# Four edits to a one-core inference step: order in two attention heads, a merged 448-column projection, and own keys placed behind the cached ones with values used in fp32

## The chip, the cores and the metric

The kernel runs on one core of a Trainium2 chip. The metric is the device time of one execution in microseconds (us). The engines are named as in the profile: PE is TensorE (PEld its weight loads), DVE is VectorE, ACT is ScalarE, POOL is GpSimd, SP is SyncE, which issues nearly all DMAs.

## The reference

One step of a two-layer streaming encoder over 512 prompt tokens and 8 running streams of 16 new tokens each (640 tokens together), width 1024, all in fp32. What matters here:

```python
# layer A, gated linear attention, 4 heads: q, k of 128, v and gate of 256 columns
q, k, v, gate, glr = split(rmsnorm(x, norm_pre) @ w_in)
g = log_sigmoid(glr @ w_gate2 + b_gate) / 16
S, o = gla_core(q * DK**-0.5, k, v, g, S0)   # chunks of 64: b = cumsum(g); (q e^b)(k e^-b)^T, causal, @ v; plus q e^b @ S
x = x + rmsnorm((rmsnorm(o, head_norm) * silu(gate)) @ w_out, norm_post)
# shared latent of layer B
lat = rmsnorm(x, kv_norm) @ kv_w_down             # 1024 x 320
ckv, krope = rmsnorm(lat[:256]), rope(lat[256:])  # keys: 512 cached + 16 own per stream
# layer B, latent attention, 8 heads
q_lat, gate = split(rmsnorm(x, norm_pre) @ w_in)  # 384 and 1024 columns
q = rmsnorm(q_lat, q_norm) @ w_uq                 # 128 + 64 rotary per head
x = x + rmsnorm((softmax(q k^T * scale + mask) v * silu(gate)) @ w_out, norm_post)
```

Outputs are the two results, the recurrent states, and the latent and rotary rows.

## The kernel before

Everything is fp32-accurate by splitting: a value x is kept as a pair, hi (x rounded to fp32r) and lo (x - hi), and a product is three matmuls, hi·hi + lo·hi + hi·lo. The helper `mm3` issues them (lines 1563 to 1565). ACT usually makes the hi half with a copy (helper `copy`, line 991) and DVE the lo half with a subtraction (helper `low`, line 1260); POOL makes some lo halves and scales weights by their norm gains.

The program is one hand-ordered list of steps, written by `steps()`, `project_out`, `latent_layer` and `samples`. `PARTS` says which engines have a part in a step, and every engine runs its parts in the order of the list, one behind the other; nothing overtakes. A wait, `after(engine, other, step)`, stands in front of a part. PE's results go to eight PSUM banks in rotation, and a step waits until the reader of the bank's last contents is done. Weights and cached rows come by SP's DMAs through a ring of stages of 1024 columns (4, and 6 in the samples; `share_stages`), in the order of `STAGED`; SP waits in order until a stage's last reader is done. A `piece` is one such load with its hi and lo copies.

Steps that the change and the prediction touch:

- Layer A, head h: `c` cumulative gates (PE), `q`, `k` projections, `kT` transposes of k (PE; its other parts write kn), `sc` scores, `U` state products of the prompt, `o` and `os` outputs of prompt and streams (os has 16 small products with the stream states), `Us` state products of the streams with a DVE add into `st_s` and ACT scalings of it, `gl(t)` output gates of the last head, `oT(t)` transposes of the gated rows. In head 0 the step `lgh(u)` makes the pair of the log gates `lg`.
- Layer B: `lc` latents (320 columns), slab `ql0` with steps `qa`, `qas` (256 columns of q_lat), slab `kq` with steps `kq`, `kqs` (64 rotary key columns and the other 128 of q_lat), `gb` gates, `cT` latent transposes.
- Samples, stream b: `ct`, `cr`, `cs` bring the cached latents transposed, the cached rotary keys and the cached latents by rows. `ss(b)` is the scores, the reduction for the maximum (DVE) and the exponentials (ACT); own keys of all streams are one block of 128 columns, where a 0 / minus-large mask product leaves only the stream's 16. `st(b)` transposes the probabilities, `sv(b)` multiplies them with the latent rows (256 columns, 5 blocks of 128 keys), `cx(b)` transposes the result. In the list, loop b holds st(b), the loads of b+3, ss(b+2), cx(b-1), sv(b).

Of the kernel before, what the change touches and what calls it, by code (L numbers as in the profile page):

```python
# [93 lines left out]
SLAB_AT["v0g"] = 3  # L94
PITCH = {name: 2 * VG if name == "v0g" else PIECE for name in SLABS}
# [22 lines left out]
def steps():  # L118
# [49 lines left out]
def project_out(out, load, ph):  # L168
# [18 lines left out]
    for t in range(NT + 4):  # L187
# [10 lines left out]
        if t == NT + 1:  # L198
            load("ql0")
# [31 lines left out]
def prompt_heads(out, load):  # L231

    for h in range(-1, HB):
        if h >= 0:
# [15 lines left out]
        if 0 <= h < 4:  # L250
            load(("hd", h + 4))
        elif h == 4:
            out += [("ct", 0), ("cr", 0)]
        elif h == 5:
            out += [("ct", 1), ("cr", 1)]


def samples(out, load):

    for b in range(SB):  # L260
        out += [("st", b)]
# [16 lines left out]
        out += [("sv", b)]  # L278
# [199 lines left out]
def program(nc, dram, outs):  # L478
# [14 lines left out]
    with ctx:  # L493
# [101 lines left out]
        cn_s = pair("cn_s", [P, KL])  # L595
# [15 lines left out]
        for i in range(NSTAGE, NWIDE):
            place[0] = qlT_at + 4 * D * (i - NSTAGE + 2)
            stage.append(sb(f"stage{i}", [P, PIECE]))
# [17 lines left out]
        spT = pair("spT", [P, TOK])  # L631
# [17 lines left out]
        sk_at = block_at[6], block_at[1]  # L649
        skS = [put(sk_at[i], f"skS{i}", [P, PAST], fp32r) for i in range(2)]  # L650
        skL = [put(sk_at[i] + 4 * PAST, f"skL{i}", [P, PAST], fp32r) for i in range(2)]
        sT_hi = [put(block_at[(5, 7)[i]], f"sT_hi{i}", [P, KC, PAST], fp32r) for i in range(2)]
        sT_lo = [put(block_at[(4, 0)[i]], f"sT_lo{i}", [P, KC, PAST], fp32r) for i in range(2)]
        cn_hi = [put(block_at[2 + i], f"cn_hi{i}", [P, PAST // P, KL], fp32r) for i in range(2)]
        cn_lo = [put((qN_at, kN_at)[i], f"cn_lo{i}", [P, PAST // P, KL], fp32r) for i in range(2)]
# [1262 lines left out]
```

How the kernel before makes its waits and increments, by code:

```python
        def after(eng, who, *step):  # L727
            eng.wait_ge(done[who], AT[who][step])
# [43 lines left out]
        @block.sync  # L773
# [58 lines left out]
                        load_stage(n)  # L832
                elif kind == "const":
                    sp.dma_start(const_raw[:, :], dram["const_r"]).then_inc(const_r_in, 16)
                elif kind == "lds":
                    h = step[1]
                    if h == 0:
                        sp.dma_start(post[:, :], dram["a_norm_post"].to_broadcast([P, D])).then_inc(post_in, 16)
                        sp.dma_start(lat_gain[:, :], dram["kv_latent_norm"].unsqueeze(0).to_broadcast([P, KL])).then_inc(post_in, 16)
                    if h:
                        sp.wait_ge(state_out, 16 * h)
                    else:
                        after(sp, "pe", "c", HA - 1)
# [18 lines left out]
                    after(sp, "dve", "r", "A", t)  # L864
                    sp.dma_start(kept[:, t, :], x1[:, t, :]).then_inc(kept_out, 16)
                elif kind == "ldk":
                    after(sp, "pe", "sv", SB - 1)
                    sp.wait_ge(kept_out, 16 * NT)
                    sp.dma_start(xB[:, :, :], kept).then_inc(rest_in, 16)
                elif kind == "och":
# [11 lines left out]
                    sp.dma_start(y_prompt[0, t * P:(t + 1) * P, :] if t < NP else y_sample.rearrange("b l d -> (b l) d"),  # L883
                                 xB[:, t, :]).then_inc(y_out, 16)
            sp.wait_ge(y_out, 16 * NT)
            sp.wait_ge(latent_out, 16 * 4)
```

## Time and profile before

| | |
|---|---|
| runs, us | 646.52, 646.67, 646.95 (median 646.67) |
| the profiled execution, us | 644.79 |
| its span, us | 643.0 |
| mean granted PE clock | 0.994 |
| PE busy, us | 617.9 (96% of the span) |
| DVE, ACT, POOL busy, us | 383.2, 315.8, 125.3 |
| DMA packets' share of 16 engines | 35.8% |

The span is the time between the first and the last instruction that the profiler saw; the execution's own time is 1.8 us longer. Busy shares are means over stages that have different limits, so each stage is looked at by itself. Matmuls overlap in the records: the time that one takes of PE is the distance from start to start, not its own length.

### The profile page before, as it was taken

The numbers are of one execution on the slowest core, as the hardware profiler recorded it, in microseconds if no ns is written. First come the engines' busy times: TensorE is split into PE (matmuls) and PEld (weight loads), VectorE is DVE, ScalarE is ACT, GpSimd is POOL, SyncE is SP. The second block draws the span as 40 slices with busy tenths as digits, with TensorE's granted clock in tenths as the row PEclk, the third lists the DMA queues.
The fourth block names the chain that finished last, engine by engine and source line by source line (L and its number), as shares of the span: only waits on it lengthen the run. The fifth ranks groups of instructions, "written<-read, shape, count | busy, mean of one in ns | idle before, by whom it ended". The sixth has DMA issues, their size and how long they took to land.

```text
span 643.0 us, 12101 instructions
## 1 busy us (share of the span) xinstructions
PE 617.9 (96%) x4714; PEld 596.3 (93%) x4714; DVE 383.2 (60%) x574; ACT 315.8 (49%) x618; POOL 125.3 (19%) x140
## 2 busy tenths in 40 slices
PE   8998999999999879999999999999999999999996
PEld 7998999999999779999999999989999888899996
DVE  5475667355454674238664567557778877773415
ACT  6786464442462553236435433355555668872311
POOL 0110010010030152216425410211000118650001
PEclk9999999999999989999999999999999999999998
DMA  8923262270262262234234420321001046766004
GB/s 301 345 82 92 90 199 73 87 215 28 74 197 67 74 229 66 86 87 173 67 93 112 127 66 2 114 70 47 34 18 50 13 151 209 252 196 229 2 1 165
DMA packets 66281, 73.69 MB, mean 115 GB/s; under 512 B 8112, under 2 KB 58544, under 8 KB 66096
## 3 DMA queue, kind: packets, MB, share of 16 engines
q1 hardware_dynamic: 66224, 72.91, 35.8%
q8 instruction: 38, 0.62, 0.4%
q14 instruction: 19, 0.16, 0.1%
HBM read 62.12 MB, written 10.78 MB: 113 GB/s over the span
## 4 chain that ended last, share of the span: by engine, by line
PE 65%; DVE 15%; ACT 10%; issue 4%; DMA 3%; POOL 2%; SPq 1%; DVEq 0%; ACTq 0%; POOLq 0%
PE bank L1563 21%; PE bank L1564 20%; PE bank L1565 20%; DVE slab_lo L1260 2%; DMA x_nat<-in_x_sample_dram 2%; ACT prob L1194 2%; DVE pT_lo L1260 2%; ACT slab_hi L991 1%; PE bank L1610 1%; DVE sT_lo L1260 1%; ACT sT_hi L991 1%; ACT qS L991 1%; DVE stat L1540 1%; DMA x_raw<-in_xT_dram 1%; DVE rows L1256 1%
## 5 line engine op out<-in xcount | busy, mean ns | idle before, releaser
L1563 PE MATMUL bank<-slab_hi,hat_hi 128*128 128x256 f32 (+2 forms) x600 | 171.0, 285 | 3.8 <-DVE rows L1423 1.8
L1564 PE MATMUL bank<-slab_lo,hat_hi 128*128 128x256 f32 (+2 forms) x600 | 169.8, 283 | 0.0
L1565 PE MATMUL bank<-slab_hi,hat_lo 128*128 128x256 f32 (+2 forms) x600 | 169.8, 283 | 0.0
L1563 PEld LDWEIGHTS bank<-slab_hi,hat_hi 128*128 128x128 f32 x600 | 115.2, 192 | 5.0 <-DVE rows L1423 2.0
L1564 PEld LDWEIGHTS bank<-slab_lo,hat_hi 128*128 128x128 f32 x600 | 115.2, 192 | 0.0
L1565 PEld LDWEIGHTS bank<-slab_hi,hat_lo 128*128 128x128 f32 x600 | 115.2, 192 | 0.0
L1260 DVE TENSOR_TENSOR slab_lo<-stage,slab_hi 128x1024 fp32r<-128x1024 f32 (+3 forms) x70 | 84.8, 1212 | 24.9 <-ACT slab_hi L991 23.4
L1563 PE MATMUL bank<-hat_hi,slab_hi 128*128 128x320 f32 x256 | 79.8, 312 | 0.9 <-DVE rows L1487 0.8
L1565 PE MATMUL bank<-hat_hi,slab_lo 128*128 128x320 f32 x256 | 79.1, 309 | 0.0
L1564 PE MATMUL bank<-hat_lo,slab_hi 128*128 128x320 f32 x256 | 79.1, 309 | 0.0
L991 ACT ACTIVATE slab_hi<-stage 128x1024 fp32r<-128x1024 f32 (+3 forms) x70 | 71.0, 1014 | 10.2 <-issue 3.6
L1563 PEld LDWEIGHTS bank<-hat_hi,slab_hi 128*128 128x128 f32 x256 | 48.1, 188 | 1.4 <-DVE rows L1487 1.4
L1564 PEld LDWEIGHTS bank<-hat_lo,slab_hi 128*128 128x128 f32 x256 | 48.1, 188 | 0.0
L1565 PEld LDWEIGHTS bank<-hat_hi,slab_lo 128*128 128x128 f32 x256 | 48.1, 188 | 0.0
L1565 PE MATMUL bank<-slab_hi,oT_lo 128*128 128x256 f32 x160 | 45.3, 283 | 0.0
L1563 PE MATMUL bank<-slab_hi,qS 128*128 128x256 f32 x128 | 36.5, 285 | 0.0
L1564 PE MATMUL bank<-slab_lo,qS 128*128 128x256 f32 x128 | 36.2, 283 | 0.0
L945 POOL TENSOR_TENSOR stat<-stat,stat 128x1 f32<-128x1 f32 (+1 forms) x8 | 2.3, 287 | 171.4 <-ACT junk L1123 136.3
L1138 ACT ACTIVATE junk<-bank 128x256 bf16<-128x256 f32 x26 | 9.7, 383 | 50.4 <-PE bank L1565 50.4
L971 POOL TENSOR_TENSOR skL<-stage,skS 128x512 fp32r<-128x512 f32 x8 | 14.6, 1827 | 92.2 <-ACT skS L991 92.2
L1565 PEld LDWEIGHTS bank<-slab_hi,oT_lo 128*128 128x128 f32 x160 | 30.7, 192 | 0.0
L1194 ACT ACTIVATE prob<-bank,stat 128x512 f32<-128x512 f32 (+3 forms) x32 | 16.6, 523 | 19.4 <-DVE stat L1521 19.1
(340 smaller groups left out, 1434.2 us busy)
## 6 DMA issues: line engine op xcount, KB each, us to landing
stage<-in_a_w_in_dram SPq DMA_DIRECT2D x22, 512.0 KB, 5.2
stage<-in_b_w_in_dram SPq DMA_DIRECT2D x10, 512.0 KB, 3.8
st_s<-in_state_gla_dram SPq DMA_DIRECT2D x4, 1024.0 KB, 6.7
out_dram<-st_s SPq DMA_DIRECT2D x4, 1024.0 KB, 4.9
stage<-in_a_w_out_dram SPq DMA_DIRECT2D x8, 512.0 KB, 4.3
stage<-in_ckvT_dram SPq DMA_DIRECT2D x8, 512.0 KB, 4.1
stage<-in_cache_ckv_dram SPq DMA_DIRECT2D x8, 512.0 KB, 4.0
stage<-in_b_w_out_dram SPq DMA_DIRECT2D x8, 512.0 KB, 3.5
```

What stands on the lines that cost most here:

```text
L945: link(pool.tensor_tensor(r, s, S1(("rrm",), stat2)[:, t:t + m], MUL))
L971: last = pool.tensor_tensor(skL[b][:, :], staged_as(kind, step), raw(skS[b][:, :]), SUB)
L991: return act.activation(out, in_, ACT.Copy)
L1138: last = act.activation(junk[:, i * 256:(i + 1) * 256], row[:, i * 256:(i + 1) * 256], ACT.Square, accum_out=S1(("y", ph, t), t=s))
L1194: last = act.activation(prob[u][:, c0:c0 + i + 1, :], bank[:, j, 0:(i + 1) * P].rearrange("p (s n) -> p s n", n=P), ACT.Exp, bias=S1(("S", ...
L1256: return dve.tensor_tensor(out, a, b, op)
L1260: return dve.tensor_tensor(lo, full, raw(hi), SUB)
L1540: last = dve.reduce_max(S1(("ss", b), stat2), row[:, 0:TOK], AX.X, negate=True)
L1563: pe.matmul(out, a[0], b[0], start=first, stop=False)
L1564: pe.matmul(out, a[0], b[1], start=False, stop=False)
L1565: return pe.matmul(out, a[1], b[0], start=False, stop=last)
L1610: last = pe.transpose(row[:, k * P:(k + 1) * P], rows[:, t, k * P:(k + 1) * P], ident)
```

## The change

1. Head 0: the log gates' pairs are made ahead of q and k; the qk(1) piece moves behind q; `kT` moves ahead of `c(2)`.
2. Last head: `Us` keeps the PE products and the DVE add, and the ACT scalings become a step `Ux`. The order becomes Us, o, os, gl(2), Ux, gl(3), oT(0), gl(4). The POOL scaling of piece wo A 1 waits for gl(3)'s DVE part.
3. Slabs `ql0` and `kq` and their steps become one slab `krq` of 448 columns, with pieces of two row blocks each in a slab of its own (`slab[4]`), and one step per token tile. k is rotated once for all tiles by a DVE step `kr`.
4. Samples: the stream's own 16 keys are copied behind the 512 cached ones (POOL step `ot`), so the scores are two halves of 264 columns without a mask product. A POOL step `zr` zeroes the last probability block. The exponentials are two ACT instructions. `sv` takes fp32 probabilities and the cached latents in fp32 straight from their stage: one fp32 matmul per block instead of three, and no pairs of them. The ring has 8 stages, and `cs` no longer has an ACT or POOL part.

```diff
 # steps(), head 0
-    ... ("lgh", HA), ("ln", 3), ("lg", 3), ("ln", 1), ("lg", 1)]
-    out += [("g0", 3), ("g0", 4), ("c", 0), ("em",), ("e", 0), ("lgh", 1), ("piece", ("qk", 1), 0), ("q", 0), ("lgh", 2), ("lgh", 3), ("qlo", 0), ("k", 0), ("klo", 0)]
-    out += [("c", 1), ("c", 2), ("kT", 0), ("c", 3)]
+    ... ("lgh", HA), ("ln", 3), ("lg", 3), ("ln", 1), ("lgh", 2), ("lg", 1), ("lgh", 3)]
+    out += [("g0", 3), ("lgh", 1), ("g0", 4), ("c", 0), ("em",), ("e", 0), ("q", 0), ("qlo", 0), ("piece", ("qk", 1), 0), ("k", 0), ("klo", 0)]
+    out += [("c", 1), ("kT", 0), ("c", 2), ("c", 3)]
 # steps(), every head; last = last head
-        out += [("os", h), ("Us", h, 0), ("Us", h, 1), ("sts", h)]
         if last:
-            out += [("o", h), ("ldr",)]
-            out += [("gl", t) for t in range(EARLY_GATE, NT - 1)] + [("oT", 0), ("gl", NT - 1)]
+            out += [("Us", h, 0), ("Us", h, 1), ("o", h), ("os", h), ("gl", EARLY_GATE), ("Ux", h, 0), ("Ux", h, 1), ("sts", h), ("ldr",)]
+            out += [("gl", t) for t in range(EARLY_GATE + 1, NT - 1)] + [("oT", 0), ("gl", NT - 1)]
 # slabs(), latent_layer()
-    out["ql0"] = halves("b_w_in", 0, "b_norm_pre")
-    out["kq"] = [[("kv_w_down", k, k + 4, KL, ROPE, "kv_norm"), ("b_w_in", k, k + 4, 256, QL - 256, "b_norm_pre")] for k in (0, 4)]
+    out["krq"] = [[("kv_w_down", k, k + 2, KL, ROPE, "kv_norm"), ("b_w_in", k, k + 2, 0, QL, "b_norm_pre")] for k in range(0, KD, 2)]
-    out += [("lcn",)]
-    load("kq")
-    out += [("qa",), ("qas",)]
+    out += [("piece", "krq", 3), ("lcn",)]
+    out += [("krq", t) for t in range(2)]
     load(("gb", 3))
-    out += [("kq",), ("kqs",), ("cn",), ("och",), ("qs",)]
+    out += [("krq", t) for t in range(2, NT)] + [("kr",), ("cn",), ("och",), ("qs",)]
 # samples()
-        out += [("st", b)]
+        out += [("st", b)] + [("zr", b + 2)] * (b + 2 < SB)
         if b + 3 < SB:
-            out += [("ct", b + 3), ("cr", b + 3)]
-        if b + 1 < SB:
-            out += [("cs", b + 1)]
+            out += [("ct", b + 3), ("cr", b + 3), ("ot", b + 3)]
@@
-        out += [("sv", b)]
+        out += [("sv", b), ("cs", b)]
 # PE, scores and values of a stream
-                    for o, keys, kr, kl in ((bank[:, 0, :], sT, skS[b % 2][:, :], skL[b % 2][:, :]),
-                                            (bank[:, 1, 0:P], cT_s, krS[:, SEQ:TOK], krL[:, SEQ:TOK])):
+                    for half in range(2):
+                        c0 = half * (KEYS // 2)
                         for c in range(KC):
-                            mm3(o, cut(qab, A_, c, b), cut(keys, A_, c), c == 0, False)
+                            mm3(o, cut(qab, A_, c, b), cut((sT_hi[b % 2], sT_lo[b % 2]), A_, c, keys), c == 0, False)
...
-                        last = mm3(bank[:, 0, 0:KL], cut(spT, A_, slice(s * P, (s + 1) * P)), cut((cn_hi[b % 2], cn_lo[b % 2]), A_, s) if s < NT - 1 else cut(cn_s, A_, A_), s == 0, s == NT - 1)
+                        x = staged_as("cs", ("cs", b))[:, s, :] if s < NT - 1 else cn_s[:, :]
+                        last = pe.matmul(bank[:, 0, 0:KL], spT[:, s * P:(s + 1) * P], x, start=s == 0, stop=s == NT - 1)
 # ACT, exponentials of a stream
-                    last = act.activation(sprob[b % 2][:, :, :], row[:, 0:TOK].rearrange("p (s n) -> p s n", n=P), ACT.Exp,
+                    act.activation(sprob[b % 2][:, 0:NT - 1, :], row[:, FIRST_KEY:FIRST_KEY + PAST].rearrange("p (s n) -> p s n", n=P), ACT.Exp,
...
+                    last = act.activation(sprob[b % 2][:, NT - 1, b * SL:(b + 1) * SL], row[:, FIRST_KEY + PAST:FIRST_KEY + KEYS], ACT.Exp,
 # POOL
+                elif kind == "ot":
...
+                    for to, x in ((sT_hi, cT_s[0]), (sT_lo, cT_s[1])):
+                        pool.tensor_copy(to[b % 2][:, :, PAST:KEYS], x[:, :, mine])
+                    mine = slice(SEQ + b * SL, SEQ + (b + 1) * SL)
+                    pool.tensor_copy(skS[b % 2][:, PAST:KEYS], krS[:, mine])
+                    last = pool.tensor_copy(skL[b % 2][:, PAST:KEYS], krL[:, mine])
```

Where the steps move, the instruction lists show the following. First DVE in head 0, before; `lg_lo` are the log gates' lo halves, `tmp` the scaled q, `slab_lo` the piece, `kt` the scaled k:

```order
L1315 SCALAR_TENSOR_TENSOR rows<-rows,bank 128x256 x2
L1260 TENSOR_TENSOR lg_lo<-z_min,lg_hi 128x512
L1260 TENSOR_TENSOR slab_lo<-stage_49,slab_hi 128x1024
L1342 SCALAR_TENSOR_TENSOR tmp<-bank,Ep 128x640
L1348 COPY q_own<-tmp 128x4x16 x2
L1260 TENSOR_TENSOR lg_lo<-z_min,lg_hi 128x512 x2
L1260 TENSOR_TENSOR qT_lo<-tmp,qT_hi 128x640
L1256 TENSOR_TENSOR kt<-bank,Em 128x640
```

The same place of the changed kernel:

```order
L1284 TENSOR_TENSOR lg_lo<-z_min,lg_hi 128x512
L1339 SCALAR_TENSOR_TENSOR rows<-rows,bank 128x256
L1284 TENSOR_TENSOR lg_lo<-z_min,lg_hi 128x512
L1339 SCALAR_TENSOR_TENSOR rows<-rows,bank 128x256
L1366 SCALAR_TENSOR_TENSOR tmp<-bank,Ep 128x640
L1372 COPY q_own<-tmp 128x4x16 x2
L1284 TENSOR_TENSOR qT_lo<-tmp,qT_hi 128x640
L1284 TENSOR_TENSOR slab_lo<-stage_49,slab_hi 128x1024
L1280 TENSOR_TENSOR kt<-bank,Em 128x640
```

All `lg_lo` now stand ahead of `tmp`, and between `tmp` and `kt` are only the lo halves of q and of the piece. Second, ACT in the last head, before; `st_s` are the stream states, `junk,stat` the squares of os (one) and o (four), `st_in` the gates' tanh:

```order
L1123 ACTIVATE junk,stat<-bank 128x256
L1127 ACTIVATE st_s<-st_s,Ep 128x256 x8
L1121 ACTIVATE junk,stat<-bank 128x256 x4
L1101 ACTIVATE st_in<-bank,stat_68 128x256 x2
L991 ACTIVATE hat_hi<-bank 128x8x128
```

And of the changed kernel:

```order
L1156 ACTIVATE junk,stat<-bank 128x256 x4
L1158 ACTIVATE junk,stat<-bank 128x256
L1136 ACTIVATE st_in<-bank,stat_68 128x256
L1163 ACTIVATE st_s<-st_s,Ep 128x256 x8
L1136 ACTIVATE st_in<-bank,stat_68 128x256
L1020 ACTIVATE hat_hi<-bank 128x8x128
```

The squares stand ahead of the eight scalings, and the tanh of gl(3) behind them. Third, POOL in the samples, before, over three streams; `cn_lo` is the lo half of the cached rows, `skL` that of the cached rotary keys:

```order
L971 TENSOR_TENSOR skL_153<-stage_130,skS_151 128x512
L967 TENSOR_TENSOR cn_lo_161<-stage_49,cn_hi_159 128x1024
L971 TENSOR_TENSOR skL_154<-stage_52,skS_152 128x512
L967 TENSOR_TENSOR cn_lo_162<-stage_129,cn_hi_160 128x1024
L971 TENSOR_TENSOR skL_153<-stage_49,skS_151 128x512
```

And of the changed kernel, over one stream:

```order
L1001 MEMSET sprob_145 128x128
L979 TENSOR_TENSOR skL_157<-stage_131,skS_155 128x512
L989 COPY sT_hi_151<-cT_s_hi 128x2x16
L989 COPY sT_lo_153<-cT_s_lo 128x2x16
L991 COPY skS_155<-krS 128x16
L992 COPY skL_157<-krL 128x16
```

One large instruction of a stream is gone, and a memset and four small copies are added, the copies behind `skL`.

## Rows read from the trace of the kernel before

**Rows 1.** Page, shares of the chain that ended last

```profile
PE 65%; DVE 15%; ACT 10%; issue 4%; DMA 3%; POOL 2%; SPq 1%; DVEq 0%; ACTq 0%; POOLq 0%
```

**Rows 2.** Waits of PE over the span: total, times, longest

```profile
PE bank L1610 <- DVE rows L1423: 4.3, 1, 4.3
PE bank L1563 <- DVE rows L1423: 1.8, 1, 1.8
PE bank L1664 <- DVE kt L1256: 1.2, 1, 1.2
```

**Rows 3.** Table by windows around head 0: window, length, busy (x), clock, DMA

```profile
48.76:55.84 7.08, 7.08 (x50) 7.08 (x50) 3.31 (x6) 4.08 (x9) 0.00 (x0) 1.00 0.10 19
55.84:65.76 9.92, 7.62 (x65) 7.25 (x64) 5.57 (x8) 6.04 (x18) 0.00 (x0) 1.00 0.58 190
```

**Rows 4.** Timeline of DVE in head 0: start, length

```profile
52.61 1.23 DVE L1260 TENSOR_TENSOR slab_lo<-stage,slab_hi 128x1024 fp32r<-128x1024 f32 x1 [0.43 <-ACT slab_hi L991]
...
56.62 1.42 DVE L1260 TENSOR_TENSOR lg_lo<-z_min,lg_hi 128x512 fp32r<-128x512 f32 x2 [1.60 <-ACT lg_hi L991]
58.94 0.82 DVE L1256 TENSOR_TENSOR kt<-bank,Em 128x640 f32<-128x640 f32 x1
```

**Rows 5.** Table by windows in head 3

```profile
212.17:238.60 26.43, 19.94 (x165) 18.30 (x164) 16.64 (x21) 14.12 (x30) 11.27 (x12) 0.94 0.54 185
230.00:232.00 2.00, 2.00 (x10) 2.00 (x11) 1.97 (x2) 0.01 (x1) 1.92 (x2) 0.50 1.01 385
229.96:235.07 5.11, 5.11 (x33) 5.11 (x34) 4.97 (x5) 1.02 (x1) 4.87 (x4) 0.72 1.01 400
235.07:238.60 3.53, 3.53 (x34) 3.41 (x32) 2.71 (x5) 2.81 (x4) 1.11 (x1) 1.00 0.12 48
```

**Rows 6.** Timeline of DVE in head 3

```profile
219.60 2.48 DVE L1256 TENSOR_TENSOR st_s<-bank,st_s 128x1024 f32<-128x1024 f32 x2
...
230.30 2.10 DVE L1256 TENSOR_TENSOR rows<-rows,st_in 128x256 f32<-128x256 f32 x1
```

**Rows 7.** Timeline of ACT in head 3

```profile
220.92 3.45 ACT L1127 ACTIVATE st_s<-st_s,Ep 128x256 f32<-128x256 f32 x8 [4.24 <-DVE st_s L1256]
```

**Rows 8.** Timeline of POOL in head 3

```profile
228.25 7.93 POOL L924 TENSOR_TENSOR stage<-stage,gain_a_head_norm 128x1024 f32<-128x1024 f32 x4 [0.22 <-POOL stat L948]
```

**Rows 9.** Table by windows: products of 256, 192, 320 and 512 columns

```profile
316.00:330.39 14.39, 14.39 (x123) 14.39 (x121) 10.88 (x9) 3.74 (x12) 8.94 (x8) 1.00 0.15 43
330.39:343.77 13.38, 13.38 (x122) 13.38 (x121) 4.26 (x9) 3.74 (x12) 0.00 (x0) 1.00 0.36 93
343.77:350.82 7.05, 7.05 (x50) 7.05 (x49) 3.08 (x12) 4.64 (x10) 5.78 (x7) 1.00 0.47 139
420.83:429.02 8.19, 8.19 (x39) 6.76 (x37) 6.18 (x8) 5.60 (x8) 0.67 (x1) 1.00 0.39 108
```

**Rows 10.** The fp32 products of line 1597: ns min, median, max, first and last start

```profile
L1597 PEld LDWEIGHTS bank<-q_own x4: 190/190/191, 4.2 to 4.8; 128*128 128x128 f32 x4
```

**Rows 11.** Table by windows in the samples

```profile
532.16:579.50 47.34, 44.53 (x327) 41.20 (x326) 35.13 (x50) 38.38 (x57) 29.60 (x14) 1.00 0.73 225
544.54:547.42 2.88, 2.88 (x20) 2.54 (x19) 2.17 (x5) 2.75 (x5) 1.85 (x1) 1.00 0.92 325
```

**Rows 12.** Timeline of ACT in two streams

```profile
551.92 0.71 ACT L991 ACTIVATE spT_hi<-bank 128x640 fp32r<-128x640 f32 x1
...
556.21 0.80 ACT L1229 ACTIVATE sprob<-bank,stat 128x640 f32<-128x640 f32 x1 [0.73 <-DVE stat L1540]
...
557.54 0.71 ACT L991 ACTIVATE spT_hi<-bank 128x640 fp32r<-128x640 f32 x1
```

**Rows 13.** Timeline of DVE in one stream

```profile
554.03 1.23 DVE L1260 TENSOR_TENSOR sT_lo<-stage,sT_hi 128x1024 fp32r<-128x1024 f32 x1
555.29 0.83 DVE L1540 TENSOR_REDUCE stat<-bank 128x1 f32<-128x640 f32 x1
```

**Rows 14.** Timeline of POOL in one stream

```profile
554.52 1.88 POOL L971 TENSOR_TENSOR skL<-stage,skS 128x512 fp32r<-128x512 f32 x1 [1.27 <-ACT skS L991]
```

More of the change, by code:

```diff
@@ L197, in project_out @@
             out += [("rx", t - 1)]
-        if t == NT + 1:
-            load("ql0")
+        if t > NT:
+            out += [("piece", "krq", t - NT - 1)]
         if 0 <= t - 4 < NT:
@@ L608, in program @@
         place[0] = qlT_at
+        slab[4] = pair("slab4", [P, KD * KRQ])
+        assert place[0] <= temp_at
+        kr_raw = thb[:, NT * ROPE:].rearrange("p (t n) -> p t n", n=ROPE)
+        place[0] = qlT_at
         y_rows = sb("y_rows", [P, NT, D])
         sprob = [sb("sprob0", [P, NT, P])]
[L611 to L613 removed]
+        for i in range(2):
+            place[0] = qlT_at + 4 * D * (i + 2)
+            stage.append(sb(f"stage{NSTAGE + i}", [P, PIECE]))
         place[0] = qS_at
@@ L630, in program @@
         place[0] = temp_at
-        spT = pair("spT", [P, TOK])
+        spT = sb("spT", [P, TOK])
         place[0] = prob_at
@@ L647, in put @@
             return sb(name, shape, dt)
[L649 to L655, printed above, removed]
+        wide = 4 * KC * KEYS
+        sT_hi = [put(block_at[(4, 0)[i]], f"sT_hi{i}", [P, KC, KEYS], fp32r) for i in range(2)]
+        sT_lo = [put(block_at[4] + (wide, 3 * wide)[i], f"sT_lo{i}", [P, KC, KEYS], fp32r) for i in range(2)]
+        skS = [put((block_at[4] + 2 * wide, block_at[0] + wide)[i], f"skS{i}", [P, KEYS], fp32r) for i in range(2)]
+        skL = [put((block_at[4] + 2 * wide + wide // 2, qlT_at + 1024)[i], f"skL{i}", [P, KEYS], fp32r) for i in range(2)]
+        assert block_at[4] + 4 * wide <= phase_at and block_at[0] + wide + wide // 2 <= block_at[2] and 1024 + wide // 2 <= 4 * D
+        for i, at in enumerate((qN_at, kN_at)):
+            stage.append(put(at, f"stage{NSTAGE + 2 + i}", [P, PIECE]))
         place[0] = lat_gain_at
@@ L963, in _ @@
                     last = pool.tensor_scalar(r, r, 1.0 / D, EPS, MUL, ADD)
-                elif kind == "cs":
-                    after(pool, "act", *step)
-                    b = step[1] % 2
-                    last = pool.tensor_tensor(cn_lo[b][:, :, :], staged_as(kind, step), raw(cn_hi[b][:, :, :]), SUB)
                 elif kind == "cr":
@@ L1203, in _ @@
                     else:
-                        after(act, "pe", "O", (1, 4)[b])
-                    last = copy(sT_hi[b % 2][:, :, :], staged_as(kind, step))
+                        after(act, "pe", "O", 4 + b)
+                    last = copy(sT_hi[b % 2][:, :, 0:PAST], staged_as(kind, step))
                 elif kind == "cr":
@@ L1516, in _ @@
                     b = step[1]
-                    last = low(sT_lo[b % 2][:, :, :], staged_as("ct", step), sT_hi[b % 2][:, :, :])
+                    last = low(sT_lo[b % 2][:, :, 0:PAST], staged_as("ct", step), sT_hi[b % 2][:, :, 0:PAST])
                 elif kind == "S":
@@ L1725, in _ @@
                     last = pe.transpose(bank[0:ROPE, 1, 0:P], krn[:, t, :], ident)
-                elif kind in ("qa", "qas"):
-                    last = natural(row, "ql0", range(NP) if kind == "qa" else [NP], 256, KD, hat)
-                elif kind in ("kq", "kqs"):
-                    last = natural(row, "kq", [NP] if kind == "kqs" else range(NP), ROPE + QL - 256, KD, hat)
+                elif kind == "krq":
+                    t = step[1]
+                    w = [x[:, 0:KD * KRQ].rearrange("p (k n) -> p k n", n=KRQ) for x in weights("krq")]
+                    for k in range(KD):
+                        if t == 0 and k % 2 == 0:
+                            after(pe, "dve", "piece", "krq", k // 2)
+                        last = mm3(bank[:, 0, 0:KRQ], cut(hat, A_, k, slice(t * P, (t + 1) * P)), cut(w, A_, k), k == 0, k == KD - 1)
                 elif kind == "qT":
```

181 lines of the change are left out of this document (97 added, 84 removed), and 4 rows, old and new, of the table PARTS.

## Prediction

> **What bounds the kernel now.** I read the shares of the chain that ended last first: 65% of it is PE, 15% DVE and 10% ACT [rows 1]. So PE's own work is the bound almost everywhere, and the rest are places where PE waits for a chain through ACT and DVE. The waits of PE say where: 4.3 us and 1.8 us once each for DVE's `rows` in the last head, and 1.2 us for `kt` in head 0 [rows 2]. Then each edited place was read for itself: tables by windows give PE's time of a stretch, timelines of the other engines say what stood in front of the late instruction. Two kinds of gain follow: less PE work (edits 3 and 4) and shorter waits (1 and 2), and I cost them apart.
>
> **Edit 1, head 0.** k's 48 products take 7.08 us, back to back [rows 3]. The next 9.92 us (c(1), c(2), kT, c(3), sc, U) are 9.92 us long for products that, at 0.1 to 0.125 each, are some 7.0 us of work: 30 for c and 5 for kT at about 0.11, 27 for sc and U at 0.12, from the 0.12 of a 256-column product below. So 2.9 us are waits; the row of `kt` is one, 1.2 us. Why `kt` is late is in DVE's timeline: the last product of k is through at 55.84, but DVE first makes two `lg_lo` (1.42 us, from 56.62), then q's lo half, and `kt` starts only at 58.94 [rows 4]. The second wait, ahead of U, comes from ACT: `kn_hi` is queued behind the copies of c(1) and c(2). After the change the `lg_lo` are done ahead of q, where DVE has room, and `kt` can start when k is through, at about 56.15; kT's transposes follow at 57.1, and c(2) and c(3) then lie over the chain kt, kT_hi, kT_lo. The price is that the two `lg_lo` and the earlier q now fall in k0's time, and that the piece's `slab_lo` (1.23 us [rows 4]), which k needs, is behind q. I put 0.1 us of delay to k's start for it. With kT at 57.1, transposes 0.5, c(2) and c(3) 2.3, sc 1.6 and U 1.5, U ends at 63.0 instead of 65.76. Gain 2.8; bounds 1.2 (only the `kt` wait goes) and 2.9 (all waits go).
>
> **Edit 2, last head.** From the first product of os to the first of `y` A are 26.43 us at a mean clock of 0.94 [rows 5]. Off it go the two waits, 4.3 and 1.8, together 6.15. PE's clock is 0.50 (the 1.2 GHz level) at 230 to 232, just after the long wait in which PE did nothing. In the 5.11 us from oT(0) on, 8 transposes and 24 products stand [rows 5]; at 3.53/32 = 0.11 per transpose and 0.12 per product they would be 3.76. So the slow stretch costs 1.35 us, and it goes if the long wait goes. The work left is 26.43 - 6.15 - 1.35 = 18.9.
>
> Why PE waits: ACT makes eight scalings of the stream states (3.45 us from 220.92), and these wait for DVE's adds (2.48 us from 219.60) [rows 6, 7]; only behind them come the four squares of o, POOL's norm chain of 1.9 us and DVE's `rows`, for which oT(0) waits. In the new order the squares come first. Step by step, from 212.17: Us and o take 3.9 us, os 1.6, so squares end near 218.3, POOL's chain near 220.2, DVE's adds also at 220.2 and its five `rows` at 222.4; PE has gl(2) and gl(3), 48 products or 5.8 us, until 223.5, so oT(0) starts without a wait. What is late next is ACT's tanh of gl(3), behind the scalings: gl(2) ends at 220.6, tanh 0.5, scalings 3.45, tanh 0.5, so 225.1, then hat_hi. gl(4) covers PE until 227.2, and the last transposes and the start of `y` may wait some 0.4 to 1.3 us for the hats. So 19.3 to 20.2, a gain of 6.2 to 7.1. I take 6.7. POOL's scaling of the weight piece (7.93 us for four [rows 8]) now starts behind gl(3)'s DVE part. It matters since the add `rows<-rows,st_in` beside it took 2.10 us [rows 6] where the other adds of this size took about 0.43.
>
> **Edit 3, krq.** The 120 products of 256 columns and their neighbours take 14.39 us, 0.120 each; the 120 of 192 columns take 13.38, 0.1115 each [rows 9]. The trace has no product of 448 columns. It has 320 columns (7.05/48 = 0.147) and 512 columns (8.19/36 = 0.2275) [rows 9]. The line between gives 0.147 + 128 x 0.00042 = 0.2006. 120 of those are 24.1, against 27.8: gain 3.7, and I add 0.1 for one change of step less and take 3.8. Bounds: 0.2275 for each (27.3, gain 0.5) would need 448 columns to cost what 512 do, which the step from 256 to 320 columns speaks against; I keep 3.3 to 4.0. The pieces come from the same stages, with ACT and DVE halves of 896 columns; the fourth lands under the first tiles. DVE's work for k moves behind the last tile as one step, and `cT` waits for it; the gb(3) products lie over it, so I cost it at nothing; if the cover were gone it would be about 2 us.
>
> **Edit 4, samples.** Eight loops take 47.34 us, 5.92 each [rows 11]. PE's work in one: scores 2.88 [rows 11], sv 15 x 0.12 = 1.8, st 0.46, cx 0.16, together 5.3. After: scores are 16 products of 264 columns, 0.123 each by the line above, 1.98, so 0.9 less. For sv only the start of the kernel has fp32 products of 256 columns: their loads are at 4.2 to 4.8, 0.20 apart [rows 10], and ten records stand for six products, so two records or about 0.41 to 0.43 per product, five make 2.1: 0.3 more. The work of a loop is then 4.7.
>
> The Trainium skill ("FP8 and Floating Point Precision", TensorE Precision Notes) says that a true fp32 product takes four passes through the array. By that rule a block would cost four times the 0.12 of a fp32r product, 0.48, and sv 2.4; the sum would be 0.3 us longer for each stream that has no cover. The trace's row is lower than that, and it decides.
>
> But PE's work does not set the loop. ACT and DVE do, in their own order: spT_hi (0.71), sT_hi (1.06), then DVE's sT_lo (1.23) and the maximum (0.83), then ACT's exponential (0.80 and a read of 0.2), qab_hi (0.4) and the next spT_hi, 5.62 us later [rows 12, 13]. The change takes 0.12 off the maximum, puts 0.15 on the exponentials (a second ACT instruction with its own read) and lets sT_lo start 0.2 earlier, since spT_lo is gone: about 5.45. cn_hi (1.06) and cn_lo are off this cycle: ACT's cn_hi lay in the time in which ACT waited for the maximum. So a loop gains about 0.2 where the cycle binds, some 0.7 in all; the last two streams have no scores behind them and pay the 0.3 of sv in full, 0.6. I take a gain of 0.1. Bounds: +5.6 (all loops at PE's 4.7 and a little) if the cycle is wrong, and -4, below.
>
> **Sum.** 2.8 + 6.7 + 3.8 + 0.1 = 13.4 off the profiled 644.79 is 631.4. The profiled execution is 1.9 below the median of 646.67, so the median forecast is 633.3.
>
> **Rivals.**
> *B, samples follow PE.* The removal of three pair makings and a DVE instruction frees more than the cycle above says, and most loops fall by 0.4 to 0.5 more, 3 to 4 us: 629.5. For it: all engines have less to do. Against: the four instructions of the cycle all stay.
> *C, own keys come late.* POOL has `skL` of 1.88 us [rows 14] and behind it four copies. The nearest POOL rows of small size are 0.2 to 0.3 us, so about 1.1 for four; PE's ss(b+2) waits for the last one. I find 0.6 us of slack. If the copies are 0.3 dearer each, each loop loses 0.5: 8 x 0.5 = 4, so 637.3.
> *D, the last head gives part back.* DVE's adds into `st_s` now stand ahead of `rows`, and POOL's scaling, beside gl(4)'s add, doubles its time or worse, as the 2.10 us shows; the hats come 2 us later: 635.5. The Trainium skill ("GPSIMD Engine Reference", Specifications) names this contention, for DVE instructions with two SBUF inputs; the row agrees.
> *E, slower.* SP takes its waits in order. The load of piece wo B 0 now waits for sv(0), and the loads of ct(5), cr(5), cs(2), ct(6) are behind it; with cached rows read by PE straight from their stage, a stage is free only after sv(b). If each loop waits for a load issued that late, PE idles from there. To lose all 13.4 us, six to eight loops must each be 1.7 to 2.3 us late. By my order of issues the nearest load, cs(2), lands 1 us early, so this needs an error of 3 us per loop: 648.
> *F, edit 1 or 3 does nothing:* if in head 0 only the `kt` wait goes, 634.9; that is inside the forecast's range.
>
> **How the numbers follow.** Forecast case 0.52, B 0.15, C 0.16, D with F 0.12, E 0.05. The forecast case alone is 631.5 to 635. The range reaches to B below and to C above: 629.5 to 637.3, leaving out E and the far ends of B and C. A measurement of this kernel can tell about 0.2% (1.3 us) from no change. All cases but E are faster by more than that: 0.94; within, 0.02; slower, 0.04.
>
> **What would show it.** In the profile after: in head 0 `kt` starts about 0.3 us behind k's last product and U ends 2.8 us earlier; in the last head no wait over 1 us at oT(0), and a granted clock of 1.00 there; krq has 120 products 0.20 apart; scores of a stream take 2.0 and sv 2.1 us of PE, and the loop stays near 5.45, with PE waiting for ACT's spT. I am wrong if fp32 products are further apart than 0.48, if 448 columns take the time of 512, if PE waits in the samples for `ot` or for a DMA, or if the clock falls in the last head all the same.

## The result and the profile after

The changed kernel took 623.69 us (median of 5, 623.65 to 624.23), the kernel before 646.52 in the same comparison (645.73 to 646.95): a ratio of 0.9649, 95% interval 0.9636 to 0.9663. That is 22.8 us; I had forecast 13.4 and a range that ended at 629.5. The direction is right, the time is outside the range.

The page of the changed kernel: span, busy times, and the granted clock in 40 slices.

```profile
span 621.9 us, 11803 instructions
...
PE 600.5 (97%) x4546; PEld 577.2 (93%) x4546; DVE 370.1 (60%) x573; ACT 307.9 (50%) x616; POOL 111.1 (18%) x173
...
PEclk9999999999999999999999999999999999999999
```

The span fell by 21.1 us, from 643.0. The two traces were then cut at the same places of PE's program, from the first instruction to the last. The numbers are us between these places; the third and fourth columns belong to experiments below.

```
                                before  changed  before+64 B  changed+64 B
start to the end of U, head 0    65.76    62.77        65.81         62.35
to the first product of y A     172.84   162.85       171.70        166.10
to the last transpose of x       71.14    68.29        68.25         70.60
to gb(3,0) (krq, or ql0 and kq)  34.02    30.93        33.84         30.78
to st(0)                        188.39   188.68       188.64        188.80
to so (the samples)              53.30    52.54        52.98         52.79
to the end                       57.54    55.85        55.82         57.21
span                            643.0    621.9        637.0         628.6
```

Two stretches whose products no edit touches, the output product of layer A (to the last transpose of x) and the end, are 2.85 and 1.7 us shorter. That was in no term of the sum. Where it comes from is seen in a table by windows over 20 us of products of 256 columns, the same code in both (y A); (x) counts instructions. The kernel before:

```profile
250.00:270.00 20.00, 20.00 (x169) 20.00 (x168) 6.29 (x7) 7.92 (x24) 5.17 (x3) 1.00 0.17 53
```

The changed kernel:

```profile
250.00:270.00 20.00, 20.00 (x179) 20.00 (x178) 7.21 (x8) 8.82 (x26) 2.22 (x4) 1.00 0.18 47
```

PE is busy throughout in both, at a clock of 1.00. Yet it starts 179 products instead of 169: by their starts they are 0.1133 us apart in the mean instead of 0.120.

**Head 0.** The windows of k and of what follows to U's end, against [rows 3], and DVE's `kt`, against [rows 4]:

```profile
48.53:55.64 7.11, 7.11 (x49) 7.11 (x49) 4.29 (x7) 3.98 (x10) 0.00 (x0) 1.00 0.01 2
55.64:62.77 7.13, 7.13 (x64) 7.02 (x63) 3.36 (x5) 4.35 (x15) 0.00 (x0) 1.00 0.73 229
```

```profile
55.90 0.82 DVE L1280 TENSOR_TENSOR kt<-bank,Em 128x640 f32<-128x640 f32 x1 [0.56 <-PE bank L1583]
```

k's products take the same, what follows 7.13 instead of 9.92 us. `kt` starts 0.26 us behind k's last product.

**Last head.** Windows over the last head, from its first product (now of Us) to the first of `y` A, against [rows 5]; the scalings and the tanh of gl(3) on ACT, against [rows 7]; the adds and the second adds of gl(3) and gl(4) on DVE, against [rows 6]:

```profile
206.46:225.62 19.16, 17.73 (x165) 16.46 (x165) 14.12 (x22) 14.17 (x30) 6.74 (x11) 1.00 0.46 139
218.00:226.00 8.00, 8.00 (x73) 7.88 (x72) 5.74 (x10) 6.62 (x11) 4.26 (x3) 1.00 0.64 203
```

```profile
216.50 3.45 ACT L1163 ACTIVATE st_s<-st_s,Ep 128x256 f32<-128x256 f32 x8
219.98 0.47 ACT L1136 ACTIVATE st_in<-bank,stat 128x256 f32<-128x256 f32 x1
```

```profile
213.65 2.48 DVE L1280 TENSOR_TENSOR st_s<-bank,st_s 128x1024 f32<-128x1024 f32 x2 [1.27 <-PE bank L1583]
...
221.02 0.43 DVE L1280 TENSOR_TENSOR rows<-rows,st_in 128x256 f32<-128x256 f32 x1
...
223.36 0.42 DVE L1280 TENSOR_TENSOR rows<-rows,st_in 128x256 f32<-128x256 f32 x1
```

The last head takes 19.16 us instead of 26.43. The clock is 1.00; no wait over 1 us is left at oT(0) or behind it (one of 1.4 us for `st_lo` ahead of o is new), and ACT's tanh of gl(3) does come right behind the scalings. The add of gl(3) took 0.43 us, not 2.10: POOL's scaling begins at 221.58, behind it. The add of gl(4) took 0.42: it starts 0.1 us ahead of the end of one of POOL's instructions.

**krq.** 120 products of 448 columns:

```profile
300.05:324.85 24.80, 24.80 (x123) 22.53 (x122) 8.79 (x17) 5.88 (x13) 5.16 (x4) 1.00 0.35 93
```

24.80 / 120 = 0.2067 each.

**Samples.** The eight loops, one stream's scores and one stream's values, against [rows 11]:

```profile
513.52:560.09 46.57, 41.75 (x281) 38.12 (x279) 28.10 (x49) 31.97 (x64) 14.08 (x36) 1.00 0.63 211
525.58:527.61 2.03, 2.03 (x18) 2.03 (x17) 1.23 (x4) 1.96 (x3) 0.21 (x1) 1.00 0.99 367
527.90:530.14 2.24, 2.24 (x12) 1.94 (x12) 2.21 (x2) 1.43 (x2) 0.64 (x1) 1.00 1.09 374
```

Scores take 2.03 us and values 2.16 (the window of values is longer by one wait of 0.08). A loop takes 46.57/8 = 5.82 us in the mean, against 5.92. Then ACT at the same place of three loops and its exponential, against [rows 12], DVE's first instruction behind the maximum, POOL's skL and its last copy, and PE's scores that follow it:

```profile
527.64 1.06 ACT L1020 ACTIVATE sT_hi<-stage 128x1024 fp32r<-128x1024 f32 x1
...
531.05 0.69 ACT L1251 ACTIVATE sprob<-bank,stat 128x512 f32<-128x512 f32 x1 [1.69 <-DVE stat L1559]
...
533.26 1.06 ACT L1020 ACTIVATE sT_hi<-stage 128x1024 fp32r<-128x1024 f32 x1
...
538.70 1.06 ACT L1020 ACTIVATE slab_hi<-stage 128x1024 fp32r<-128x1024 f32 x1
```

```profile
532.60 0.42 DVE L1284 TENSOR_TENSOR qab_lo<-bank,qab_hi 128x256 fp32r<-128x256 f32 x1 [1.63 <-ACT qab_hi L1020]
```

```profile
529.50 1.84 POOL L979 TENSOR_TENSOR skL<-stage,skS 128x512 fp32r<-128x512 f32 x1 [3.48 <-ACT skS L1020]
...
531.85 0.20 POOL L992 CAST skL<-krL 128x16 fp32r<-128x16 f32 x1
```

```profile
532.30 0.36 PE L1581 MATMUL bank<-sT_hi,qab_hi 128*128 128x264 f32 x1 [1.46 <-POOL sprob L1001]
```

From one sT_hi to the next are 5.62 us, and to the instruction at that place in the loop after, a piece's slab_hi, 5.44. ACT waits 1.69 us for DVE's maximum and then DVE 1.63 us for ACT's qab_hi: the two wait for each other. PE waits 1.46 us for the copies. The row names the memset `sprob` that stands behind them, but in the program PE waits for the copies, and it starts 0.25 us behind the last one. The waits of PE in this part of the trace, and who released it by the profile:

```profile
PE bank L1581 <- POOL sprob L1001: 2.9, 3, 1.5
PE bank L1581 <- ACT sprob L1253: 2.4, 3, 1.6
```

Two of the three waits put down to ACT also end 0.25 us behind the last copy (537.73 and 544.44). None of PE's waits here is for a DMA.

### The profile page after: what moved, and what is told of

It reads as the page before. It is cut to its first block and busy times, and to the rows that moved or that the text cites. A ratio compares the mean times of both kernels' runs of the same rounds, so it can differ in the third digit from the quotient of the medians.

```text
span 621.9 us, 11803 instructions
## 1 busy us (share of the span) xinstructions
PE 600.5 (97%) x4546; PEld 577.2 (93%) x4546; DVE 370.1 (60%) x573; ACT 307.9 (50%) x616; POOL 111.1 (18%) x173
## 5 line engine op out<-in xcount | busy, mean ns | idle before, releaser
L1581 PE MATMUL bank<-slab_hi,hat_hi 128*128 128x256 f32 (+2 forms) x560 | 160.6, 287 | 2.0 <-DVE hat_lo L1284 1.0
L1582 PE MATMUL bank<-slab_lo,hat_hi 128*128 128x256 f32 (+2 forms) x560 | 159.6, 285 | 0.0
L1583 PE MATMUL bank<-slab_hi,hat_lo 128*128 128x256 f32 (+2 forms) x560 | 159.6, 285 | 0.0
L1581 PEld LDWEIGHTS bank<-slab_hi,hat_hi 128*128 128x128 f32 x560 | 105.3, 188 | 3.8 <-DVE slab_lo L1284 1.4
L1583 PEld LDWEIGHTS bank<-slab_hi,hat_lo 128*128 128x128 f32 x560 | 105.6, 189 | 0.8
L1582 PEld LDWEIGHTS bank<-slab_lo,hat_hi 128*128 128x128 f32 x560 | 105.2, 188 | 0.7
```

Source lines behind the costliest of these rows:

```text
L1581: pe.matmul(out, a[0], b[0], start=first, stop=False)
L1582: pe.matmul(out, a[0], b[1], start=False, stop=False)
L1583: return pe.matmul(out, a[1], b[0], start=False, stop=last)
```

## The experiments

Three questions were open: what makes unchanged products start closer together; whether each edit is worth its term; and what sets the samples' loops. The kernel before was timed beside each group and took 646.98 (644.61 to 648.82), 648.17 (644.55 to 648.20) and 648.24 (646.05 to 648.79). Its mean clock in these executions goes with its time: 0.994 in those of 644.6 to 645.3, 0.987 to 0.990 in those of 645.9 to 647.9, 0.984 to 0.986 in those above 648. The groups e, f and g ran on three different chips; where runs of two groups are compared, a part of the difference may be the chip's.

**Where tiles lie.** Edit 4 made the constants shorter and two small tables longer, so `hat`, `qS`, `oT_lo` and everything behind `junk` moved by 1472 bytes in SBUF, while the slabs stayed. Worked out from the allocations, `hat` lay 0 modulo 128 bytes from the slabs before, and lies 64 modulo 128 now. In a product of 256 columns `hat` is the stationary side and the slab streams. Four kernels have nothing but unused bytes added:

```diff
+        place[0] += 64          # e1 on the kernel before; e3 on the changed kernel
+        place[0] += 32          # e2 on the kernel before; g4 on the changed kernel
         rows_at = place[0]
-        place = [-(-nc.sbuf_base // 64) * 64]
+        place = [-(-nc.sbuf_base // 64) * 64 + 64]      # e4 on the changed kernel: all tiles
```

**e1**, the kernel before with 64 bytes:

> The kernel before, with 64 unused bytes ahead of `rows`, so that `rows`, `hat` and everything behind lies 64 bytes later in SBUF and the weight slabs do not; nothing else is changed. Theory A (addresses): in the changed kernel the 256-column products run 113 ns apart instead of 120 ns because its constants are smaller and so `hat`, qS and oT_lo lie at another offset to the slabs (64 instead of 0 modulo 128 bytes). Then this kernel gets the 113 ns too, and about 7 to 8 us over some 1150 ns-priced groups of products: 638.5 to 639.5 against 646.5. Theory B (the lower spacing comes from less work on DVE, ACT, POOL or from another chip): 120 ns stay, 646.5 within 1 us.

Measured: 638.97 (638.58 to 641.63), ratio 0.9886 (0.9855 to 0.9917). The same window of its trace:

```profile
250.00:270.00 20.00, 20.00 (x179) 20.00 (x178) 8.20 (x8) 7.12 (x18) 3.89 (x3) 1.00 0.21 61
```

**e2**, 32 bytes in the kernel before:

> The kernel before with 32 unused bytes ahead of `rows`. Theory A does not say which offsets are good. If any offset other than 0 modulo 128 gives 113 ns: 639. If only 64 does: 646.5. If an offset that is no multiple of 64 costs more than either: above 646.5. Theory B: 646.5.

Measured: 644.31 (642.25 to 646.66), ratio 0.9953 (0.9933 to 0.9973), and the products with `hat` are 117 ns apart in the median, but 118.3 in the mean. The kernel before has 119.9 in the mean, e1 115.1. So 32 bytes give about a third of what 64 give.

**e3**, the changed kernel put back to distance 0:

> The changed kernel with 64 unused bytes ahead of `rows`, which puts `hat`, qS and oT_lo back to offset 0 modulo 128 to the slabs. Theory A: products of 256 columns 120 ns apart again, 630.5 to 632 against 623.7 (my forecast of the edits alone was 633.3). Theory B: 623.7 within 1.

Measured: 630.67 (630.44 to 631.14), ratio 0.9752 (0.9723 to 0.9780). The products are 118.7 ns apart in the mean, not quite the 119.9 of the kernel before at the same distance (171 instead of 169 in the window):

```profile
250.00:270.00 20.00, 20.00 (x171) 20.00 (x170) 4.10 (x4) 5.49 (x19) 3.72 (x2) 1.00 0.24 66
```

**e4**, the changed kernel moved as a whole:

> The changed kernel with all tiles, the slabs too, 64 bytes later. If the distance between the stationary tile and the moving slab counts, it is as in the changed kernel: 623.7, 113 ns. If the stationary tile's own address counts (a multiple of 128 is bad), 120 ns and about 631. Theory B: 623.7.

Measured: 623.48 (623.41 to 623.76), ratio 0.9639 (0.9616 to 0.9662). Moving all tiles together by 64 bytes changes nothing, so it is the distance and not the address that counts.

**g4**, the distance of 96:

> The changed kernel with 32 unused bytes ahead of `rows`: the stationary tiles lie 96 modulo 128 bytes from the slabs (64 now, 0 in the kernel padded by 64, which took 630.67, 32 in the padded kernel before, whose products were 117 ns apart). If 96 is like 32: 117 ns apart and about 627. If only the distance 0 is bad: 623.7. If 64 is the only good one: 630.7.

Measured: 629.87 (629.55 to 633.40), ratio 0.9735 (0.9707 to 0.9763), its products 118.5 ns apart in the mean: 96 is as bad as 0. The window has the same 171 products as e3's, and of the 0.8 us by which the kernel is faster than e3, 0.5 lie in krq (30.26 against 30.78), where the distance isn't changed.

```profile
250.00:270.00 20.00, 20.00 (x171) 20.00 (x170) 4.10 (x4) 5.12 (x17) 3.79 (x2) 1.00 0.25 69
```

Theory A holds and B falls: 64 bytes give the kernel before 7.5 us and take 7.0 from the changed one, without one instruction more or less. Of the distances tried, 64 is the only good one; 32 gives a little, and 0 and 96 can't be told apart. The distance is not all of it: the kernel before and e3 have the same distance and are 1.2 ns apart for each product, some 1.6 us over the 1409 products of the changed kernel, and the cause of that is open. A check within one kernel: in e1 the samples' fp32r values have both sides moved, so their distance is 0 as before, and they stay 120 ns apart.

**Each edit.** Here are edits put alone on e1, and all but edit 4. Their diffs are those of the change: steps() in head 0 for f1, steps() in the last head with `Ux` for f2, slab `krq` with its steps for f3, all three for f4. e1 ran on another chip than f1 to f4. Against the kernel before of their own groups the ratios are 0.9886 for e1, 0.9815, 0.9808, 0.9867 and 0.9652 for f1 to f4, so by them f1 to f4 gain 4.6, 5.0, 1.2 and 15.1 us more than e1 does.

**f1**:

> The kernel before with the 64 unused bytes ahead of `rows` (alone it took 638.97) and edit 1, head 0's order, alone. My term of 2.8 us: 636.2. If only the wait for `kt` goes: 637.8. The changed kernel's trace puts U's end 3.0 us earlier: 636.0.

Measured: 635.20 (634.61 to 635.67), ratio 0.9815 (0.9779 to 0.9852); clock 0.994 in all four executions. That is 3.8 us less than e1. In its trace U ends 2.1 us earlier (63.69 against 65.81), though PE had come 0.5 us later than in e1 to the products of `glT` (33.45 against 32.95), ahead of the steps that edit 1 moves.

**f2**:

> The same padded kernel with edit 2, the last head's order, alone. My term of 6.7 us: 632.3, granted clock 1.00 in the last head. Rival D (the adds ahead of `rows` and POOL's scaling give 2 us back): 634.3.

Measured: 634.39 (633.63 to 635.68), ratio 0.9808 (0.9775 to 0.9840), a gain of 4.6 only; clock 0.987 to 0.990. In its trace the stretch from U's end in head 0 to y A is 163.32 us against 171.70 in e1, 8.4 less. Of these about 1.6 are that e1 had lost more to the clock in the last head than the kernel before in its trace: 28.0 us from os to y A against 26.43 [rows 5]. So the median meets rival D's 634.3 by luck: the last head has what the changed kernel has (19.17 us), and what is missing is lost in head 0. Head 0 itself is 4.6 us longer (70.42 against 65.81). The clock was 0.50 in it twice, from 34 to 41 us and from 65 us on:

```profile
34.00:40.00 6.00, 6.00 (x26) 6.00 (x26) 4.07 (x8) 5.32 (x8) 2.48 (x1) 0.50 0.05 19
```

**f3**:

> The same padded kernel with edit 3, the 448-column products, alone. My term was 3.8 us against products of 256 columns that were 120 ns apart. With those at 113 ns already, the 256-column half is 0.8 us cheaper, so 3.0 is left: 636.0. If 448 columns cost what 512 do: 639 or more.

Measured: 638.41 (637.75 to 639.00), ratio 0.9867 (0.9836 to 0.9899), a gain of 0.6; clock 0.985 to 0.988. Its krq stretch is 30.30 us against 33.84, a gain of 3.5; head 0 is again longer (68.06), with a clock of 0.50 from 60.3 to 70.5 us.

**f4**:

> The same padded kernel with edits 1, 2 and 3, that is the changed kernel but for the samples. If the edits add up: 638.97 - 3.0 - 6.7 - 3.0 = 626.3, and edit 4 is then worth 2.6 against the changed kernel's 623.7. If edit 4 is worth the 0.8 us that the two traces differ by between the first st and the last sv, this one takes 624.5.

Measured: 624.15 (623.84 to 625.61), ratio 0.9652 (0.9620 to 0.9683), so edit 4 without its addresses is worth 0.5, near the trace's 0.8 in the samples (53.34 against 52.54) and far from 2.6. The three edits together gain 14.8 on e1, alone they sum to 8.9. The traces say where the rest is: f4's is shorter than e1's by 3.3 us to U's end, 8.9 from there to y A and 3.0 in krq. f2 and f3 have the same last head and krq, but lose 4.6 and 2.3 us in head 0 to the clock, which e1's trace does not, though its order there is the same.

**Head 0 and the clock.** So the old order was put back into the changed kernel:

```diff
-    ... ("ln", 3), ("lg", 3), ("ln", 1), ("lgh", 2), ("lg", 1), ("lgh", 3)]
-    out += [("g0", 3), ("lgh", 1), ("g0", 4), ("c", 0), ("em",), ("e", 0), ("q", 0), ("qlo", 0), ("piece", ("qk", 1), 0), ("k", 0), ("klo", 0)]
-    out += [("c", 1), ("kT", 0), ("c", 2), ("c", 3)]
+    ... ("ln", 3), ("lg", 3), ("ln", 1), ("lg", 1)]
+    out += [("g0", 3), ("g0", 4), ("c", 0), ("em",), ("e", 0), ("lgh", 1), ("piece", ("qk", 1), 0), ("q", 0), ("lgh", 2), ("lgh", 3), ("qlo", 0), ("k", 0), ("klo", 0)]
+    out += [("c", 1), ("c", 2), ("kT", 0), ("c", 3)]
```

**g3**:

> The changed kernel with head 0's order of before. Edit 1 alone in its trace is worth 3.0 us: 626.7 if the clock is no matter. If head 0's waits are also what lets the clock fall there in most executions of the kernel before (0.984 to 0.990 for the whole, against 0.994 where it did not fall), it falls here too, and the median is 1.5 to 3.5 us higher, 628.2 to 630.2, with more spread and clocks of 0.990 to 0.995 against 0.997 to 0.999.

Measured: 628.30 (626.18 to 630.07), ratio 0.9701 (0.9677 to 0.9725). The five clocks are 0.990, 0.990, 0.992, 0.992 and 0.997, and the time follows them: 629.55 and 630.07 at 0.990, 626.18 at 0.997. Windows of its trace around the 1.2 us wait for `kt`, which ends at 59.5:

```profile
56.00:60.00 4.00, 2.48 (x22) 2.26 (x21) 3.03 (x4) 1.30 (x3) 0.00 (x0) 1.00 0.57 216
60.00:64.00 4.00, 4.00 (x23) 4.00 (x21) 1.65 (x2) 3.56 (x14) 0.00 (x0) 0.54 0.21 34
64.00:68.00 4.00, 4.00 (x22) 4.00 (x22) 1.15 (x3) 1.64 (x4) 0.00 (x0) 0.61 0.69 228
```

PE is busy for 2.48 of 4 us, and then the clock is 0.50 from 60.6 to 67.5. In the traces of e2 and f3 it falls at the same place, for 10.2 us. f2's first fall, at 34 us, is another: it comes ahead of the steps that edit 1 moves, behind waits of 0.4 and 0.9 us, of which the changed kernel has the second as well. At 0.997 the difference to the changed kernel is 2.5 us, at 0.990 it is 6.1. In 25 executions of six kernels with edits 1 and 2 (the changed kernel, e3, e4, f4, g4 and below g2) the clock was 0.997 to 0.999 but for two (0.994 and 0.991).

**What sets the samples' loops.**

```diff
-                    for s in range(NT):
+                    for s in (0, NT - 1):                     # g1
-            out += [("ct", b + 3), ("cr", b + 3), ("ot", b + 3)]
+            out += [("ct", b + 3), ("ot", b + 3), ("cr", b + 3)]      # g2, in the other three places too
```

**g1**:

> The changed kernel with two of the five key blocks in sv: the values of cached keys 128 to 511 are left out, so PE has three fp32 products (1.3 us) less in each stream, 10.4 us in all. If the cycle of ACT and DVE sets the loops (5.44 us without a piece), only the last two streams, which have nothing else to wait for, gain: 2.6 us, 621.1. If PE sets them: up to 10 us, 613.5.

Measured: 621.55 (620.95 to 622.60), ratio 0.9596 (0.9576 to 0.9616). From st(0) to st(6) its trace has 34.1 us, the changed kernel's 35.3, with 7.8 us less of PE's work in between. Its clocks are 0.986 to 0.996, lower than the changed kernel's; in the trace the clock is 0.50 from 533.3 to 536.6, and the loop with it takes 8.0 us instead of 6.6. Even with these 1.4 us given back the six loops gain 2.6 of 7.8 us at most. The rest of the samples is 1.6 us shorter, where 2.6 were expected.

**g2**:

> The changed kernel with POOL's four copies of a stream's own keys ahead of the subtraction that makes skL, so that they are out of the chain skS, skL, copies, scores. In the trace of the changed kernel the scores start 0.25 us behind the last copy, in three of the loops, so if POOL's chain sets the loops each gains up to 0.65 us, 3 to 5 us in all: 619 to 621. If the cycle of ACT and DVE sets them: 623.7 within 0.5.

Measured: 623.38 (623.26 to 627.00), ratio 0.9641 (0.9609 to 0.9673). PE's waits in the samples:

```profile
PE bank L1581 <- POOL sprob L1001: 1.7, 2, 1.0
PE bank L1861 <- DVE ctxn L1566: 1.2, 4, 0.3
PE bank L1822 <- DVE prob L1550: 1.1, 1, 1.1
PE bank L1581 <- POOL skL L979: 1.1, 1, 1.1
PE bank L1581 <- DVE pT_lo L1284: 1.0, 1, 1.0
PE bank L1581 <- ACT sprob L1253: 0.5, 1, 0.5
```

With POOL's copies out of the way PE waits less ahead of the scores (1.7, 1.1 and 0.5 us against 2.9 and 2.4) and more for `ctxn` (1.2), and the samples are hardly shorter (52.41 us against 52.54). So POOL's copies don't set the loops, and PE's work at most in part. The cycle of ACT and DVE is left, and in the trace these two wait for each other. It was not shortened by itself, so it is argued and not shown by an experiment. (g2 also moves the waits of PE and DVE from `ot` to `cr`, the step that is now last on POOL.)

## Why the prediction was wrong

**The edits' terms were nearly right.** With the distance put back (e3), the changed kernel is 14.4 us faster than before by the spans of the profiled executions, where my sum was 13.4, and its 630.67 lies in my range. That the sum is met so closely is in part luck: some 1.6 of the 14.4 come from the 1.2 ns that a product of 256 columns costs less in e3, at the same distance. Point by point:

- Edit 1: forecast 2.8, measured 3.0 in the traces (3.4 with e3). `kt` and the cover for its chain came as worked out; k started 0.2 us earlier rather than 0.1 later.
- Edit 2: forecast 6.7. From head 0 to y A e3 is 6.74 us shorter than before, but 0.66 of that are heads 1 to 3 ahead of it; the last head alone takes 20.35 us in e3, so 6.1. In the changed kernel it takes 19.16. The waits and the clock's 1.35 us went as said. Rival D's mechanism is absent in the changed kernel and there in e3: the add of gl(4) starts with one of POOL's scalings and takes 2.15 us instead of 0.42, and PE then waits 0.8 us ahead of the last transposes. In the changed kernel this add falls at the end of a POOL instruction, which is luck of timing. POOL's scaling and the add in e3:

```profile
222.99 5.90 POOL L937 TENSOR_TENSOR stage<-stage,gain_a_head_norm 128x1024 f32<-128x1024 f32 x3 [4.83 <-DVE rows L1281]
```

```profile
224.99 2.15 DVE L1281 TENSOR_TENSOR rows<-rows,st_in 128x256 f32<-128x256 f32 x1
```

- Edit 3: forecast 3.8, measured 3.1. The step that was mis-sized is "0.147 + 128 x 0.00042 = 0.2006": 448 columns took 0.2067, above the line through 320 and 512 columns by 3%. The added 0.1 was there: the stretch is 3.09 us shorter, its 120 products 2.97. `krq` is laid behind `rows` like `hat`, so by the allocations its distance is 0 modulo 128 in every kernel that has it. Whether 64 would make it cheaper wasn't tried; at this one distance it took 0.207 in e3 and e4 too, but 0.203 in f3 and g4.
- Edit 4: forecast 0.1, measured 0.8 in the trace and 0.5 by f4. The 5.45 us of the ACT-DVE cycle was met in a loop without a piece (5.44), as were 2.0 for the scores and 2.1 for the values (2.03, 2.16). Rival B had the loops follow PE: g1 speaks against it. Rival C's mechanism is there, and with it a sign that I had named for being wrong, PE waiting for `ot`; the wait for spT that I had expected isn't. But the four copies took 0.64 us, where I had 1.1, and g2 says that the loops are no longer for them. Rival E didn't happen: PE waits for no DMA there.
- The Trainium skill's four passes for an fp32 product ("FP8 and Floating Point Precision", TensorE Precision Notes): the trace agrees roughly. A product of 256 columns took 0.433 us, which is four times 0.108, or 3.8 times the 0.1133 of an fp32r product at the good distance; my 0.48 multiplied the rule with the 0.12 of a product that was slowed by its distance.

**The step that failed, 7 us.** I took it that a product which the change leaves alone costs what it did ("the 0.12 of a 256-column product below", and no term for layer A's output product or the end). The change moved the stationary tiles by an odd multiple of 64 bytes against the slabs, and the products of 256 columns of `hat`, `qS` and `oT_lo` with a slab got cheaper: 0.1133 us instead of 0.120 in y A, 114.9 ns instead of 119.9 in the mean of all with `hat`. The move is worth the 7.0 us between e3 and the changed kernel. It was to be seen: the diff shrinks the constants, and the tiles are placed one behind another. I read the diff's step lists and not its addresses.

**The second step, about 2 us.** "The profiled execution is 1.9 below the median of 646.67, so the median forecast is 633.3": I carried this offset to the changed kernel. It was no constant. It is clock that falls in most executions of the kernel before and didn't fall in the profiled one. That it falls in head 0 is inferred: no trace of that kernel has it, but those of e2, f2, f3 and g3 do, which have the same order there. Edit 1 takes away the waits in front of it. In the changed kernel the profiled execution is the median. So edit 1 was worth 3.0 us in the profile and 4.6 in the medians (628.30 against 623.69). That head 0's old order brings the lower clock is shown by g3. That it is by the waits fits f1, f3, g3 and f2's second fall, but not f2's first one; which of the waits it hangs on wasn't tried.

**Together.** 633.3 less 7.0 for the distance, 1.9 for the offset and 1.0 for the terms is 623.4, against 623.69 measured. The 1.0 has in it the 1.6 us of cheaper products in e3, so the terms themselves were some 0.6 us too large.

**Open.** Why a distance of 64 bytes modulo 128 between the stationary and the streamed tile is good isn't settled. The products of 320 columns, where the slab is stationary and `hat` streams, stayed 147 ns apart at either distance. So the rule found here holds for the one kind of product. What makes the same product cost 119.9 ns in the kernel before and 118.7 in e3 is open too.

## What to carry to other kernels

When an edit changes the size of any tile, look where the others move to, and compare the spacing of products that the edit doesn't touch: the first sign was a shorter stretch without an edit in it. 64 unused bytes are a cheap experiment on a kernel that is bound by matmuls. And the offset between a profiled execution and the median is to be explained (here by the granted clock) before it is carried over, for a change may remove its cause.

## What the runs showed of the hardware

- Products of 128x128 by 256 columns in fp32r, back to back, in y A: 0.1133 us apart with the stationary and the streamed tile 64 modulo 128 bytes apart (e1, e4, the changed kernel); 0.120 (before) and 0.1187 (e3) at 0, 0.1187 at 96 (g4), 0.1183 at 32 (e2).
- Products of 448 columns: 0.2067 us apart (0.203 in f3 and g4); an fp32 product of 256 columns 0.433, in two records of 0.216.
- An add of two SBUF tiles on DVE took 2.15 us where it started together with a POOL instruction of 1.9 us (e3), and 0.42 where it started 0.1 us ahead of the end of one.
- Waits of about 1 us in head 0 were followed by a granted clock of 0.50 for 7 to 10 us in the traces of e2, f2, f3 and g3, and not in those of the kernel before and e1, which have the same waits. Times of the kernel before spread over 4.3 us with its mean clock.
